# First layer of a two-stage model on one core: the dense groups in another order, the recurrence's preparation between them, norms on 128 rows

## The chip, the cores and the metric

The kernel runs on one core of a Trainium2 chip. The metric is the device time of one execution in microseconds (us), the median of several runs. TensorE does the matmuls, VectorE and ScalarE the elementwise work (ScalarE also the functions such as exp and gelu), GpSimd builds masks, and SyncE issues the loads from HBM. Each engine runs its own instructions strictly in the order in which they are written; they meet at semaphores.

## The reference

The input is one sequence of 512 tokens with 1024 channels. The change is in the mixer of the first layer; the 32-expert stage and the second model half behind it are not touched.

```
h = modulate(rmsnorm(x), shift1, scale1)          # shift1 and scale1 are columns of c @ ada_w + ada_b
z = h @ w_in                                      # split in zu, zv (512 each), then r, k, v (512 each), xw 32, xa 32, xg 96
# spatial half
u = gelu(zu);  v = layernorm(gelu(zv)) * ln_w + ln_b
y_a = u * (tril(ws) applied over the 128 tokens of a chunk, by head, to v, + bs)
# recurrent half: z + (z shifted by a token - z) * mu, then
decay = exp(-exp(-softplus(-(w0 + tanh(xw) @ w2)) - 0.5));  a = sigmoid(a0 + xa @ a2);  g = sigmoid(xg) @ g2
kk = k * k_k, divided by its norm over the 64 channels of a head;  k = k * (1 + (a - 1) * k_a)
state = state * decay + (state . -kk) (kk * a) + v k      # by head, token after token;  y = state . r
y_b = (norm of y by head * gn_w + gn_b + sum(r * k * r_k) * v) * g
x = x + gate1 * (concat(y_a, y_b) @ w_out)
```

## The kernel before

**Layout.** Activations lie transposed: channels on the 128 partitions, the 512 tokens along the row. A tile is 128 x 512; `R`, `K`, `V`, `KK`, `A` (the rate a), `C` (the decay) and `E` (scratch) have four tiles each. A chunk is 128 tokens. Eight heads of 64 channels make two heads per tile.

**Dense groups.** `PLAN` lists units of weights of at most 1 MB; SyncE loads them in that order into a ring of four slots. A `dense` group is 256 output channels: 2 x 8 x 3 = 48 matmuls of 128x128 by 512 (three because weight and activation are each split in a rounded high part and a rest). ScalarE writes the high part of a unit and VectorE the rest; the pair is called a *cut* here (`cut`, ordered by `Ahead`, which cuts a unit or two ahead of its use, and for which ScalarE waits until the unit two before it is used up). A group's result lies in one of two halves of `psD` in turn. For r, k, v and the two low-rank groups `lora_wa` and `lora_g` (24 matmuls each), ScalarE and VectorE each make a pass over the result (the token shift: L2150 or L2157, then L2333 or L2345).

**Small results.** Everything else that TensorE makes goes through `psA`, four banks in the fixed turn of `aux_plan`. TensorE waits on a bank until its previous content is taken.

**Order in the first layer.** Modulation rows (eight 1 MB units, `modulation`), their 16 columns (`to_column`), the norm, then the dense groups zv, zu, r, k, v, lora_wa, lora_g. Then comes the preparation of the recurrence: the low-rank products (`wl`, `al`), k times its factor, the squared norm of kk by head (`kn`, a product with the block matrix `blk`, so that all 64 rows of a head hold the same sum), root and reciprocal of it, the bonus (`bon`), the spatial mix (`gm`), the running sum of the decay, three exponentials, and the products `AR`, `A`, `K` that the chunks read. Then four chunks, each with seven levels of a block inversion, `u0`, `sa`, `y` and `st`. Last the norm of y by head (`gnm`, `gnv`), the gate `gg`, and the groups `w_out`. `keep_clock` runs matmuls whose result nobody reads.

Of the kernel before, what the change touches and what calls it, by code (L numbers as in the profile page):

```python
# [118 lines left out]
def gm2(a):  # L119
    out = np.zeros((P, 4, 512), np.float32)  # L120
    bs = np.asarray(a["gmlp_bs"][0])
    for j in range(4):
        for o in range(2):
            out[64 * o:64 * o + 64, 0, P * j:P * j + P] = bs[2 * j + o]
    out[0:32, 1] = np.asarray(a["rwkv_w2"][0])
    out[32:64, 2] = np.asarray(a["rwkv_a2"][0])
    out[0:96, 3] = np.asarray(a["rwkv_g2"][0])
    return out.reshape(P, UNIT)
# [12 lines left out]
def dense_plan():  # L141
# [10 lines left out]
    for j in range(8):  # L152
        mat(("ada", j), "ada_w", 0, cols(256 * j, 256 * j + 256))
    for h in range(2):
        mat(("zv",), "w_in", 0, cols(512, 1024), 4 * h, 4)
    for name, lo in (("zu", 0), ("r", 1024), ("k", 1536), ("v", 2048)):
        for j in range(2):
            mat((name, j), "w_in", 0, cols(lo + 256 * j, lo + 256 * j + 256))
    mat(("lora_wa",), "w_in", 0, cols(2560, 2624))
    mat(("lora_g",), "w_in", 0, cols(2624, 2720))  # L160
# [56 lines left out]

GROUPS = [g for g in dict.fromkeys(p[0] for p in PLAN) if g[0] not in ("ada", "zv")]
GROUPS = [("zv", 0), ("zv", 1)] + [q for g in GROUPS for q in ([(*g, h) for h in range(4)] if g[0] == "ple_w" else [g])]
# [3 lines left out]
def aux_plan():  # L223

    a = [("mr", 0, 0), ("mr", 0, 1), ("ss", 1)] + [("mr", 0, j) for j in range(2, 8)] + [("mod",)]
    a += [("wl", j) for j in range(4)] + [("al", j) for j in range(4)]
    a += [("kn", j) for j in range(4)] + [("bon", j) for j in range(4)]
    a += [("gm", c) for c in range(4)]
    for c in range(NCH):
# [13 lines left out]
        a += [("u0", c), ("sa", c), ("y", c)] + ([("st", c)] if c < NCH - 1 else [])  # L243
    a += [("gnm", j) for j in range(4)] + [("gnv", j) for j in range(4)] + [("gg", j) for j in range(4)]
# [72 lines left out]
def build(nc, x_t, params, w_dense, p_t, w_moe, out_t, stop=None):  # L317
    ctx = ExitStack()
    with ctx:
# [41 lines left out]
        X, H, YC = area(0, 8), area(4096, 8), area(8192, 8)  # L361
        XF, HF, YF = flat(0, 4096), flat(4096, 4096), flat(8192, 4096)
        o = 12288
        R, K, V, KK, A, C, E = (area(o + 2048 * i, 4) for i in range(7))
        RF, KF, VF, KKF, AF, CF, EF = (flat(o + 2048 * i, 2048) for i in range(7))
# [5 lines left out]
        T1 = area(sp + 1536, 1)  # L371
        NB = area(sp, 4)
        small = flat(sp + 4864, 512)
        stat = small[:, 0:4]
        AR = HF.rearrange("p (j c a t) -> p j c a t", j=4, c=4, a=2)
# [71 lines left out]
        g1_at, g2_at = ((RAW + 2 * (SPLIT_NO[last_unit((g,))] % 2)) * UNIT for g in ("lora_g", "lora_wa"))  # L447
# [3 lines left out]
        VTMP = flat(sp + 2816, 2048)  # L451
# [5 lines left out]
        YC_P = parts(o, o + 4 * 2048, 8)  # L457
        XI, XT = EF[:, 0:1024], EF[:, 1024:2048]
        AB = RF.rearrange("p (h a t) -> p h a t", h=8, a=2)
        AK = KKF.rearrange("p (h a t) -> p h a t", h=8, a=2)  # L460
# [184 lines left out]
        def moe_pool(pool, step):  # L645

            partial_sum(pool, step, [YC[:, k, :] for k in range(6)], PRE2, "sq2", 0)
# [39 lines left out]
        def moe_act(act, step, root, ahead, x_hi):  # L687

            for k in range(KT):
                act.wait_ge(sem("x_mixed"), k + 1)  # L690
                act.activation(YC[:, k, :], X[:, k, :], ACT.Square).then_inc(sem("sq2"), 1)
# [307 lines left out]
        def moe_tensor(pe, aux, filled, dense, colsum, product, keep_clock, spread):  # L999
            out = aux(("ss", 2))  # L1000
            for k, src in enumerate([PRE2, YC[:, 6, :], YC[:, 7, :]]):
# [994 lines left out]
        def _(sp_):  # L1996
            sp_.dma_start(XF, x_t).then_inc(sem("x_in"), 16)
            sp_.dma_start(par[:, :], params).then_inc(sem("par_in"), 16)

# [12 lines left out]
            for i in range(N_FIRST):  # L2012
                load(i)
                if PLAN[i][0] == ("lora_g",):

                    for n, g in ((1, "lora_wa"), (0, "lora_g")):
                        at = g1_at if n == 0 else g2_at
                        sp_.wait_ge(sem("units_done"), last_unit((g,)) + 1)
# [13 lines left out]
        def _(pool):  # L2032
# [17 lines left out]
            for i, m in enumerate(level):  # L2050
# [7 lines left out]
                                        pattern=[[2 * b, P // (2 * b)], [0, b]], channel_multiplier=-1))  # L2058
            pool.nop().then_inc(sem("consts"), 1)
# [6 lines left out]
            pool.wait_ge(sem("v_centred"), 1)  # L2066
            for m in range(4):
                step(pool.tensor_tensor(VTOK[:, m, :], VTOK[:, m, :], G1[:, 1024:1536], ALU.mult))
                pool.tensor_tensor(VTOK[:, m, :], VTOK[:, m, :], G1[:, 1536:2048], ALU.add)\
                    .then_inc(sem("v_norm"), 1)  # L2070
# [9 lines left out]
        def _(act):  # L2080
# [19 lines left out]
            ahead.limit = last_unit(("lora_g",))  # L2100
# [5 lines left out]
            act.activation(YF, XF, ACT.Square).then_inc(sem("sq1"), 1)  # L2106
            act.wait_ge(sem("par_in"), 16)
# [12 lines left out]
            ahead(last_unit(("zv",)))  # L2120

# [6 lines left out]
            for h in range(2):  # L2128
                ahead.enter(("zv", h))
                group_ready(act, ("zv", h))  # L2130
                act.activation(VTOK[:, 2 * h:2 * h + 2, :], dbank(("zv", h)), ACT.Gelu_apprx_tanh)\
                   .then_inc(group_freed(("zv", h)), 1)
            ahead.leave(("zv", 1))
            for h in range(2):
                ahead.enter(("zu", h))
                group_ready(act, ("zu", h))
                act.activation(YC[:, 2 * h:2 * h + 2, :], dbank(("zu", h)), ACT.Gelu_apprx_tanh)\
                   .then_inc(group_freed(("zu", h)), 1)
                ahead.leave(("zu", h))
            root(small[:, 48:52])  # L2140
# [710 lines left out]
```

## Time and profile before

| | us |
|---|---|
| median of 3 runs | 2892.51 (2889.79 to 2893.48) |
| the profiled execution, its own time | 2894.15 |
| its span in the trace | 2892.4 |
| TensorE busy in the span | 2665.4 (92%) |
| VectorE busy | 1576.2 (54%) |
| ScalarE busy | 1143.5 (40%) |
| mean granted TensorE clock | 0.955 |

The span is cut into 40 slices in the profile; a slice is 72.3 us long. The first layer takes the first eight and a half of them. The lines below the head are the busy share of each slice in tenths and the granted clock in tenths of full speed:

```
PE   7884999679999999989988799999999999999998
DVE  2248555547888888854357654333345474333334
PEclk8986999899999999999998899999999999999999
```

A digit says how busy an engine is, not whether anyone waits for it; waits are read in the timeline of the engine.

### The profile page before, as it was taken

What the parts mean: (1) busy time and instruction counts of PE and PEld (TensorE: products, weight loads), DVE (VectorE), ACT (ScalarE), POOL (GpSimd) and SP (SyncE); (2) the same over time, 40 slices, a digit from 0 to 9 for tenths busy, and PEclk for the clock granted to TensorE, in tenths of its full rate; (3) what the DMA queues carried; (4) which work ended last, traced back from release to release, by engine and by line L of the source; (5) the groups of instructions that cost most, each with busy time, mean ns of one, the idle gap of its engine ahead of it and who ended that gap; (6) DMA issues with size and microseconds to landing.
All of it is one profiled execution on the core that took longest, in us unless ns stands there. A gap on an engine that the chain in (4) does not pass through costs nothing.

```text
span 2892.4 us, 30835 instructions
## 1 busy us (share of the span) xinstructions
PE 2665.4 (92%) x12700; PEld 2081.9 (72%) x12700; DVE 1576.2 (54%) x1683; ACT 1143.5 (40%) x1322; POOL 152.1 (5%) x160
## 2 busy tenths in 40 slices
PE   7884999679999999989988799999999999999998
PEld 5653888457778878868865576888877756888876
DVE  2248555547888888854357654333345474333334
ACT  3231122235777778742231423222224364222223
POOL 1010000012111111000000000000010001000010
PEclk8986999899999999999998899999999999999999
DMA  6120222027999999952220122222232201223220
GB/s 251 55 88 15 73 74 74 0 88 270 361 361 361 361 352 363 357 209 81 95 78 11 55 77 71 88 90 102 75 108 81 79 1 66 98 71 115 80 102 30
DMA packets 64285, 388.06 MB, mean 134 GB/s; under 512 B 13328, under 2 KB 13456, under 8 KB 22288
## 3 DMA queue, kind: packets, MB, share of 16 engines
q1 hardware_dynamic: 53424, 372.41, 35.2%
q0 software_dynamic: 9280, 8.42, 0.8%
q10 hardware_dynamic: 1440, 5.24, 0.5%
q8 instruction: 102, 1.67, 0.2%
q14 instruction: 39, 0.32, 0.0%
HBM read 390.21 MB, written 20.97 MB: 142 GB/s over the span
## 4 chain that ended last, share of the span: by engine, by line
PE 76%; DVE 8%; ACT 3%; DMA 2%; issue 2%; DVEq 0%; ACTq 0%; POOLq 0%
PE psD L2579 60%; PE psA L2740 2%; DMA ring<-w_moe 2%; PE psA L2760 2%; PE psA L2754 1%; PE psA L1910 1%; DVE arena L2442 1%; PE psA L1039 1%; DVE ring_r L920 1%; PE psA L1941 1%; ACT ring_r L718 1%; PE psD L2587 1%; DVE ring_r L2279 1%; PE psA L2648 1%; PE psA L2587 1%
## 5 line engine op out<-in xcount | busy, mean ns | idle before, releaser
L2579 PE MATMUL psD<-rounded,ring_r 128*128 128x512 f32 (+1 forms) x6168 | 1456.7, 398 | 48.0 <-DVE ring_r L2279 25.3
L2579 PEld LDWEIGHTS psD<-rounded,ring_r 128*128 128x128 f32 (+1 forms) x6168 | 1158.9, 188 | 345.0 <-issue 34.9
L2279 DVE TENSOR_TENSOR ring_r<-ring,ring_r 128x2048 fp32r<-128x2048 f32 (+2 forms) x143 | 306.8, 2147 | 249.7 <-ACT ring_r L2097 245.6
L2579 PE MATMUL psD<-ring_r,rounded 128*128 128x512 f32 (+1 forms) x1728 | 410.6, 394 | 6.5 <-DVE rounded L930 3.3
L2097 ACT ACTIVATE ring_r<-ring 128x2048 fp32r<-128x2048 f32 (+2 forms) x143 | 251.7, 1761 | 397.0 <-PE psD L2579 366.6
L2579 PEld LDWEIGHTS psD<-ring_r,rounded 128*128 128x128 f32 x1728 | 318.1, 190 | 87.9 <-issue 9.1
L920 DVE TENSOR_TENSOR ring_r<-ring,ring_r 128x2048 fp32r<-128x2048 f32 x128 | 293.2, 2291 | 45.6 <-ACT ring_r L718 43.1
L718 ACT ACTIVATE ring_r<-ring 128x2048 fp32r<-128x2048 f32 x128 | 245.3, 1917 | 59.4 <-DMA ring<-w_moe 35.0
L2579 PE MATMUL psD<-rounded,rounded 128*128 128x512 f32 x768 | 191.7, 398 | 0.0
L1702 DVE TENSOR_TENSOR arena<-arena,psD 128x512 f32<-128x512 f32 x44 | 30.2, 687 | 255.2 <-ACT arena L1418 255.2
L920 DVE TENSOR_TENSOR rounded<-ring,rounded 128x2048 fp32r<-128x2048 f32 x64 | 146.5, 2289 | 23.6 <-ACT rounded L718 23.6
L2579 PEld LDWEIGHTS psD<-rounded,rounded 128*128 128x128 f32 x768 | 139.6, 188 | 27.3
L1418 ACT ACTIVATE arena<-psD 128x512 f32<-128x512 f32 x44 | 26.4, 599 | 307.9 <-PE psD L2579 307.9
L718 ACT ACTIVATE rounded<-ring 128x2048 fp32r<-128x2048 f32 x64 | 123.0, 1922 | 11.7 <-DMA ring<-w_moe 11.0
L2482 DVE TENSOR_TENSOR arena<-arena,psA 128x512 f32<-128x512 f32 x88 | 60.5, 688 | 66.0 <-PE psA L2754 47.8
L637 POOL TENSOR_TENSOR arena<-arena 128x512 f32<-128x512 f32 x5 | 7.5, 1507 | 1682.7 <-DVE arena L1675 1296.4
L2202 ACT ACTIVATE arena<-psA 128x512 f32<-128x512 f32 x56 | 33.4, 597 | 149.6 <-PE psA L2740 149.6
L2103 ACT ACTIVATE rounded<-arena 128x512 fp32r<-128x512 f32 x112 | 67.3, 627 | 61.0 <-DVE arena L1702 36.5
L1675 DVE SCALAR_TENSOR_TENSOR arena<-arena,psD 128x512 f32<-128x512 f32 x40 | 27.5, 686 | 78.7 <-PE psD L2579 78.0
L631 POOL DMA_INDIRECT pair_rows<-arena,ints x32 | 36.2, 1132 | 510.3 <-ACT arena L734 493.1
L2740 PE MATMUL psA<-arena 128*128 128x128 f32 x384 | 52.5, 285 | 1.6 <-DVE arena L2469 1.0
L2760 PE MATMUL psA<-arena 128*128 128x128 f32 x384 | 50.5, 276 | 0.0
(388 smaller groups left out, 2420.8 us busy)
## 6 DMA issues: line engine op xcount, KB each, us to landing
ring<-w_moe SPq DMA_DIRECT2D x192, 1024.0 KB, 7.3
ring<-w_dense SPq DMA_DIRECT2D x134, 1024.0 KB, 4.8
ring<-w_dense SPq DMA_DIRECT2D x16, 768.0 KB, 4.0
ring<-w_dense SPq DMA_DIRECT2D x16, 640.0 KB, 3.7
arena<-x_t SPq DMA_DIRECT2D x1, 2048.0 KB, 8.8
token_rows<-arena ACTq DMA_DIRECT2D x4, 512.0 KB, 2.6
arena<-pair_rows SPq DMA_DIRECT2D x4, 512.0 KB, 7.8
arena<-pair_rows ACTq DMA_DIRECT2D x4, 512.0 KB, 8.2
```

What stands on the lines that cost most here:

```text
L631: return pool.indirect_dma_start(pair_rows, bass.IndirectOffsetOnAxis(ap=pair_i[:, e:e + 1], axis=0), buf, None, bounds_check=2 * SEQ - 1, ...
L718: act.activation(expert_parts(E.place(j, PARTS))[0], slot_tile(slot), ACT.Copy).then_inc(sem("m_hi"), 1)
L920: dve.tensor_tensor(lo_, slot_tile(E.place(j, RAW)), hi, ALU.subtract).then_inc(sem("m_lo"), 1)
L2097: act.activation(parts_of(u, nk, nco)[0], ring_of(u, nk, nco), ACT.Copy).then_inc(sem("w_hi"), 1)
L2103: act.activation(dst, src, ACT.Identity if kw else ACT.Copy, **kw).then_inc(sem("x_hi"), 1)
L2202: act.activation(UI[:, 512 * q:512 * q + 512], bank(("u", c, lv, q)), ACT.Copy)\
L2279: dve.tensor_tensor(lo_, ring_of(u, nk, nco), hi, ALU.subtract).then_inc(sem("w_lo"), 1)
L2482: dve.tensor_tensor(buf[:, qs], buf[:, qs], bank(n_), ALU.add).then_inc(freed(n_), 1)
L2579: mm = pe.matmul(out, w[a], x[b], start=start and i == 0, stop=stop_ and i == 2)
L2587: pe.matmul(bank_, ones, masks[:, 0:SEQ], start=True, stop=True)
L2740: mm = pe.matmul(out[:, P * i:P * i + P], hs(LM[lv % 2], 4 * q + i), ident if lv == 0 else hs(XI, 4 * q + i), start=True, stop=True)
L2760: mm = pe.matmul(out[:, P * i:P * i + P], hs(UI, 4 * q + i), hs(XT, 4 * q + i), start=True, stop=True)
```

## The change

It reorders the first layer and rewrites its two norms by head.

- `PLAN`, and with it loads, cuts and matmuls, now goes k, lora_wa, r, v, lora_g, zv, zu. ScalarE and VectorE write the first two cuts between the tiles of `h1`, where both stood ahead of them.
- The preparation stands between the groups in all three engines' orders, and the exponentials come after the second v group. The factor -exp(-0.5) is now the scale of the exponentials.
- The norms by head: `by_head` gathers the sums of all eight heads and four chunks on 128 rows of 128 columns (16 matmuls with 32 output columns), root and reciprocal run on that 128 x 128 tile once, a product with the mask `PICK` spreads it to 512 columns, and `to_heads` (four matmuls, results `ks` and `gns`) brings it back to the channels.
- The 16 modulation columns are made two at a time behind each row. The 9 matmuls of `keep_clock` ahead of the first group are 3.
- The layer norm's scale and shift move from GpSimd to VectorE, with `ln_w` and `ln_b` loaded by a DMA of their own, which waits for the first four products of `AR`. A further small load (`WA2`, 256 KB) stands behind the parameters, and its end is waited for with them.
- GpSimd writes `PICK` and the map `HEADS` (7 small memsets and 4 copies of 32 x 512) before it signals `consts`, which TensorE's first matmul waits for.
- The gelu of zu, and the taking of `bon`, wait until all dense groups are done, since `YC` now lies over the split activations. The spatial mix of chunk k runs in the gaps at the end of recurrence chunks 0 and 1.

```diff
+    halves("k", 1536)
+    mat(("lora_wa",), "w_in", 0, cols(2560, 2624))
+    halves("r", 1024)
+    halves("v", 2048)
+    mat(("lora_g",), "w_in", 0, cols(2624, 2720))
     for h in range(2):
         mat(("zv",), "w_in", 0, cols(512, 1024), 4 * h, 4)
...
+    halves("zu", 0)
...
+            heads_map(HEADS)
             pool.nop().then_inc(sem("consts"), 1)
...
-                ready(dve, ("kn", j))
-                take(("kn", j), dve.tensor_scalar(NB[:, j, :], bank(("kn", j)), 1e-24, None, ALU.max))
-                counts_.append(ask_root())
...
-                inverse(counts_[j], NB[:, j, :])
-                step(dve.tensor_tensor(KK[:, j, :], KK[:, j, :], NB[:, j, :], ALU.mult))
...
+            def by_chunk():
+                inverse(ask_root(), NORM)
+                step(dve.tensor_tensor(NORM_C.rearrange("p (c t) -> p c t", c=NCH),
+                                       NORM.unsqueeze(1).to_broadcast([P, NCH, P]),
+                                       PICK[:, 0:NCH].unsqueeze(2).to_broadcast([P, NCH, P]), ALU.mult))
+                dve.nop().then_inc(sem("norm"), 1)
...
+            take(("kn",), dve.tensor_scalar(NORM, bank(("kn",))[:, 0:P], 1e-24, None, ALU.max))
+            by_chunk()
...
+            group_ready(dve, ("zu", 1))
+            for j in range(4):
+                ready(dve, ("bon", j))
+                take(("bon", j), dve.tensor_tensor(YC[:, 4 + j, :], bank(("bon", j)), V[:, j, :], ALU.mult))
...
+            def by_head(name, src, signal):
+                out = aux(name)
+                for j in range(4):
+                    pe.wait_ge(sem(signal), j + 1 if signal == "gn_sq" else 1)
+                    for c in range(NCH):
+                        mm = pe.matmul(out[32 * c:32 * c + 32, 0:P], PICK[:, 32 - 2 * j:64 - 2 * j],
+                                       src[:, j, P * c:P * c + P], start=(j == 0), stop=(j == 3))
+                filled(mm)
...
+            dense(("k", 0), hr, at="h1")
+            dense(("k", 1), hr)
+            dense(("lora_wa",), hr, (64,))
+            dense(("r", 0), hr)
+            by_head(("kn",), E, "kk_sq")
...
+            dense(("r", 1), hr)
+            to_heads("ks", HEADS, 1)
+            dense(("v", 0), hr)
...
+            dense(("v", 1), hr)
+            dense(("lora_g",), hr, (96,))
...
+            pe.wait_ge(sem("v_norm"), 4)
             pe.wait_ge(sem("bk"), 8)
...
-                inverse(counts_[j], NB[:, j, :])
-                step(dve.tensor_tensor(E[:, j, :], E[:, j, :], NB[:, j, :], ALU.mult))
-                step(dve.tensor_scalar(E[:, j, :], E[:, j, :], pc("gn_w", j), pc("gn_b", j), ALU.mult, ALU.add))
-                step(dve.tensor_tensor(YC[:, 4 + j, :], YC[:, 4 + j, :], E[:, j, :], ALU.add))
...
+                take(n_, dve.scalar_tensor_tensor(E[:, j, :], E[:, j, :], pc("gn_w", j), bank(n_),
+                                                  ALU.mult, ALU.mult))
+                step(dve.scalar_tensor_tensor(YC[:, 4 + j, :], E[:, j, :], pc("gn_b", j), YC[:, 4 + j, :],
+                                              ALU.add, ALU.add))
```

TensorE before, from the last matmuls of the last dense group (L2579) to the first chunk (L2718 on): wl, al, kn, bon and gm follow each other.

```order
L2579 MATMUL psD<-rounded_8_57,ring_r 96x512
L2694 MATMUL psA<-arena,ring 128x512 x4
L2696 MATMUL psA<-arena,ring 128x512 x4
L2699 MATMUL psA<-arena,masks 128x512 x4
L2702 MATMUL psA<-arena,masks 128x512 x4
L2708 MATMUL psA<-ring,arena 64x128 x32
L2718 MATMUL psA<-masks,arena 128x128 x12
L2728 MATMUL psA<-arena 128x256 x16
```

TensorE now, at four places of the dense stretch: the rows around the end of the first r group (by_head L2716, wl L2732, al L2734), of the second r group (ks L2723), of the first v group (bon L2740), and of the last dense group zu.

```order
L2606 MATMUL psD<-rounded_8_57,ring_r 128x512
L2716 MATMUL psA<-arena 32x128 x16
L2732 MATMUL psA<-arena 128x512 x4
L2734 MATMUL psA<-arena 128x512 x4
L2606 MATMUL psD<-rounded_8_57,ring_r 128x512
...
L2723 MATMUL psA<-arena 128x512 x4
...
L2740 MATMUL psA<-arena,masks 128x512 x4
...
L2606 MATMUL psD<-rounded_8_57,ring_r 128x512
L2774 MATMUL psA<-masks,arena 128x128 x12
L2784 MATMUL psA<-arena 128x256 x16
```

What stood in one row of small products behind the groups stands in three places between them; behind the last group the chunks' first products follow at once.

VectorE before, in the preparation: the norm of kk (L2260 the reciprocals; the last two of its four repeats are left out).

```order
L2260 RECIPROCAL arena<-arena 128x512 [waits aux_free1,root_out]
L2373 TENSOR_TENSOR arena<-arena 128x512 [waits dve_step]
L2374 TENSOR_TENSOR arena<-arena 128x512 [waits dve_step]
L2260 RECIPROCAL arena<-arena 128x512 [waits root_out,dve_step]
L2373 TENSOR_TENSOR arena<-arena 128x512 [waits dve_step]
```

VectorE now, from the shift of the first r group on: a cut (L2299) stands ahead of the norm, the reciprocal is 128 columns wide, and the shift of the second r group (L2337) follows the work on K.

```order
L2337 SCALAR_TENSOR_TENSOR arena<-psD,par,arena 128x511 [waits shift_a] x2
L2299 TENSOR_TENSOR ring_r<-ring,ring_r 128x2048 [waits shift_b,w_hi]
L2370 TENSOR_SCALAR arena<-psA 128x128 [waits aux_ready]
L2280 RECIPROCAL arena<-arena 128x128 [waits aux_free1,root_out]
L2356 TENSOR_TENSOR arena<-arena 128x512 [waits dve_step]
L2374 TENSOR_SCALAR arena<-arena,par,gain 128x512 [waits dve_step,aux_free2]
L2376 TENSOR_TENSOR arena<-arena 128x512 [waits dve_step]
```

The four wide reciprocals are gone, and the norm is now queued behind a cut, and a shift behind the norm.

## Rows read from the trace of the kernel before

**Rows 1.** Busy time by stage: columns are stretch, length, engines, granted clock, DMA.
```profile
0.00:52.50 52.50, 34.89 (x211) 20.82 (x211) 17.71 (x22) 22.35 (x27) 10.09 (x39) 0.84 0.81 329
52.50:189.50 137.00, 125.75 (x530) 98.13 (x528) 36.44 (x40) 33.39 (x35) 0.00 (x0) 0.96 0.12 44
189.50:272.90 83.40, 34.21 (x140) 19.44 (x140) 71.73 (x80) 23.46 (x27) 12.12 (x9) 0.65 0.16 63
272.90:526.50 253.60, 231.25 (x2012) 213.60 (x2012) 126.76 (x168) 51.46 (x93) 0.00 (x0) 0.93 0.20 67
526.50:564.10 37.60, 17.41 (x40) 7.52 (x41) 32.43 (x31) 10.95 (x17) 0.00 (x0) 0.80 0.00 0
```

**Rows 2.** Timeline of TensorE (start, length, instructions, wait before), 0 to 130 us.
```profile
13.35 1.94 PE L2648 MATMUL psA<-ring,par 128*32 128x256 f32 x16 [13.35 <-DMA ring<-w_dense]
...
17.20 7.13 PE L2628 MATMUL psA<-arena,masks 128*128 128x512 f32 x16
...
33.45 1.94 PE L2648 MATMUL psA<-ring,par 128*32 128x256 f32 x16 [0.50 <-DMA ring<-w_dense]
...
36.01 6.96 PE L2659 MATMUL psA<-gain,arena 128*128 128x1 f32 x32 [0.57 <-ACT arena L2112]
...
76.56 22.66 PE L2579 MATMUL psD<-rounded,ring_r 128*128 128x512 f32 x96 [1.11 <-ACT arena L2131]
```

**Rows 3.** Timeline of GpSimd, 0 to 285 us.
```profile
3.69 0.53 POOL L2041 MEMSET reset<- 128x512 f32 x1
...
12.63 0.24 POOL L2057 TENSOR_SCALAR_AFFINE_SELECT masks<-masks 128x64 f32<-128x64 f32 x1
...
196.01 1.26 POOL L2069 TENSOR_TENSOR arena<-arena,ring 128x512 f32<-128x512 f32 x1
```

**Rows 4.** Timeline of ScalarE, 0 to 285 us.
```profile
43.49 0.81 ACT L2124 ACTIVATE arena<-arena,mod,gain 128x512 f32<-128x512 f32 x1 [3.30 <-DVE gain L2302]
44.34 0.63 ACT L2103 ACTIVATE rounded<-arena 128x512 fp32r<-128x512 f32 x1
...
132.99 1.27 ACT L2150 ACTIVATE arena<-psD,gain 128x512 f32<-128x512 f32 x2 [8.07 <-PE psD L2579]
134.14 1.91 ACT L2097 ACTIVATE ring_r<-ring 128x2048 fp32r<-128x2048 f32 x1
144.19 1.27 ACT L2150 ACTIVATE arena<-psD,gain 128x512 f32<-128x512 f32 x2 [8.13 <-PE psD L2579]
...
189.60 1.28 ACT L2163 ACT_TABLE_LOAD   x1
```

**Rows 5.** Timeline of VectorE, 0 to 285 us.
```profile
136.09 2.29 DVE L2279 TENSOR_TENSOR ring_r<-ring,ring_r 128x2048 fp32r<-128x2048 f32 x1 [0.97 <-ACT ring_r L2097]
...
239.06 5.00 DVE L2388 TENSOR_TENSOR_SCAN arena<-reset,arena 128x512 f32<-128x512 f32 x4
```

**Rows 6.** Timeline of TensorE, 130 to 275 us.
```profile
231.46 5.50 PE L2702 MATMUL psA<-arena,masks 128*128 128x512 f32 x8 [21.98 <-DVE arena L2379]
236.89 3.71 PE L2708 MATMUL psA<-ring,arena 128*64 128x128 f32 x64
260.29 1.09 PE L2718 MATMUL psA<-masks,arena 128*128 128x128 f32 x4 [19.69 <-DVE arena L2428]
```

**Rows 7.** Timeline of VectorE, start of the first and the second chunk.
```profile
272.86 2.36 DVE L2454 TENSOR_TENSOR arena<-arena,masks 128x1024 f32<-128x1024 f32 x2
...
334.08 5.77 DVE L2442 TENSOR_TENSOR arena<-psA,masks 128x512 f32<-128x512 f32 x8 [0.95 <-PE psA L2728]
```

**Rows 8.** Chain of work that ended last, in order of time, 340 to 350 us.
```profile
347.42 1.00 PE psA L2648 x16
```

**Rows 9.** Timeline of VectorE, 510 to 582 us.
```profile
534.51 3.35 DVE L2260 RECIPROCAL arena<-arena 128x512 f32<-128x512 f32 x1
...
556.20 2.85 DVE L2529 TENSOR_TENSOR arena<-arena,psA 128x512 f32<-128x512 f32 x4
```

**Rows 10.** Chain of work that ended last, 560 to 612 us.
```profile
564.12 47.53 PE psD L2579 x192
```

More of the change, by code:

```diff
@@ L2099, in _ @@
             ahead = Ahead(cut)
-            ahead.limit = last_unit(("lora_g",))
+            ahead.limit = last_unit(("zu", 1))
             def x_hi(dst, src, **kw):
@@ L2221, in _ @@
                 act.activation(C[:, j, :], E[:, j, :], ACT.Square).then_inc(sem("gn_sq"), 1)
-            for j in range(4):
-                root(NB[:, j, :])
+            root(NORM)
             act.wait_ge(sem("y_halves"), 2)
@@ new lines, in to_heads @@
+            def to_heads(name, heads, count):
+                pe.wait_ge(sem("norm"), count)
+                for j in range(4):
+                    filled(pe.matmul(aux((name, j)), heads[:, P * j:P * j + P], NORM_C, start=True, stop=True))
+            dense(("k", 0), hr, at="h1")
[3 more added lines that the diff above has]
+            by_head(("kn",), E, "kk_sq")
+            pe.wait_ge(sem("lora_w"), 1)
+            for j in range(4):
+                filled(pe.matmul(aux(("wl", j)), WA2[0:32, P * j:P * j + P], LO[0:32, 0, :], start=True, stop=True))
@@ L2683, in _ @@
-            hr = tile_of(H_P)
-            for name in ("zu", "r", "k", "v"):
-                for h in range(2):
-                    dense((name, h), hr)
-            dense(("lora_wa",), hr, (64,))
-            dense(("lora_g",), hr, (96,))
-            g2, ws = G2, G1[:, 0:1024].rearrange("p (h t) -> p h t", h=8)
-            pe.wait_ge(sem("gm2_in"), 16)
-            pe.wait_ge(sem("lora_w"), 1)
-            for j in range(4):
-                filled(pe.matmul(aux(("wl", j)), g2[0:32, 1, P * j:P * j + P], LO[0:32, 0, :], start=True, stop=True))
@@ L2704, in _ @@
-            for c in range(4):
-                pe.wait_ge(sem("v_norm"), c + 1)
-                out = aux(("gm", c))
+                for b in range(2):
+                    if i == 0:
+                        pe.wait_ge(group_freed(("zv", b)), GROUP_NO[("zv", b)] // 2)
+                    for k in range(nk):
+                        for m in (2 * b, 2 * b + 1):
+                            mm = product(psD[:, GROUP_NO[("zv", b)] % 2, m % 2, :],
+                                         [v[:, 4 * i + k, P * m:P * m + P] for v in H_P],
+                                         [v[:, k, :] for v in w], i == 0 and k == 0, i == 1 and k == nk - 1)
```

378 lines of the change are left out of this document (204 added, 174 removed).

## The prediction

> **What bounds the kernel now.** I read the busy time by stage first, since the change touches only the first 611 us. Up to 52.5 us the loads of the modulation weights and the first norm set the pace. From 52.5 to 189.5 us TensorE is busy 125.8 of 137 us at a granted clock of 0.96: the dense groups. From 189.5 to 272.9 us it is busy 34.2 of 83.4 us at 0.65, while VectorE is busy 71.7: the preparation, bound by VectorE. Then come the chunks (TensorE 231 of 254), and from 526.5 to 564.1 the norm of y, where VectorE is busy 32.4 of 37.6 us [rows 1]. The timelines say who waits: TensorE waits 22.0 us for VectorE ahead of the bonus and 19.7 us ahead of the first chunk's transposes [rows 6]. In both norms a reciprocal of 128x512 stands four times on VectorE, one takes 3.35 us [rows 9]. The dense groups run evenly: ScalarE takes up a group's result every 11.20 us (132.99 to 144.19), so a matmul of 512 columns takes 11.2/48 = 0.233 us, a group of 24 takes 5.6 [rows 4].
>
> **Can the preparation lie under the groups?** By total work, yes. VectorE had 36.4 us to do in the groups' stage and 71.7 in the preparation's [rows 1]; three quarters of four reciprocals go (4 x 3.35 x 0.75 = 10 us). That leaves about 98 us for some 140 us of TensorE work. Totals don't decide it, though: the queues are strictly ordered, and a cut that is late stops TensorE. So I walked them.
>
> **Start.** TensorE's first matmul began at 13.35 us, when its weights had landed [rows 2]. It now waits for GpSimd, whose last mask ended at 12.87 [rows 3], and then 7 small memsets (0.2 us each, since the 64-column mask takes 0.24) and 4 copies of 512 columns. The trace has no such copy: at least the 0.53 us of the 512-column memset, at most the 1.26 of an operation with two inputs [rows 3]; between ends this near, I take 0.9. TensorE starts at about 18 (16.4 to 19.5), 4.6 later. The last modulation row moves from 33.45 to 38.1. Behind it 32 column instructions took 6.96 us [rows 2]; 4 are left, 0.9. With the row's 1.94, its copy and VectorE's two small operations, h1 begins at 42.2 instead of 43.5 [rows 4]. ScalarE then has 8 tiles of 0.81 + 0.63 us and 2 cuts of 1.91 (15.2 in all); the rest of the last tile 0.7 and six matmuls 1.4 make the first k group end at 59.4.  Next k (11.2), lora_wa (5.6), r (11.2, with 0.3 lost to a cut that ends late): the first r group ends at T = 87.7.
>
> **From T on.** Cover and delays, in us after T; shift on ScalarE 1.27, cut 1.91 and 2.29 [rows 4, 5].
> ScalarE ends shift and cut at 3.4, VectorE its cut at 5.7. Only then does VectorE take the gathered norm. Root, a reciprocal of 128 columns (3.35/4 = 0.84) and the mask end at 8.0. ScalarE, after the root, reloads its table (1.28 [rows 4]) and takes wl and al one by one, since the four banks turn; TensorE is through with them at 12.0, where its own work alone (gathering 2.0, eight products at 7.13/8 = 0.89 [rows 2]) was 9.1: a wait of 2.9. Gathering is 32 instructions of at most 32 output columns; 16 such take 1.00 in the chain [rows 8], so 2.0.
> Second r group to 23.2, ks (4 x 0.89) to 26.8, v to 38.0, bonus to 41.6, v to 52.8, lora_g to 58.4. VectorE meanwhile has r times r_k times k and the products with ks (done at 37.5), the four scans (5.00 [rows 5]) and the two passes behind them, done at 51.8, just ahead of the second v group's result. The exponentials follow that group's shift and cut: three at 1.9 and a table, ending at 63.2. ScalarE reaches the shift of lora_g only then, and zv's second half needs that half of psD: TensorE waits 0.8 at 64.3. zv ends at 81.9. The gelu of zv holds zu up by 1.3, much like the 1.11 wait before [rows 2]. zu ends at 105.6. The layer norm is done at 98.7 (cut, 4 statistics, root, 8 products of 0.72), so it is covered, with 7 us to spare; without that cover each us counts in full. TensorE is free for the chunks at 87.7 + 105.6 = 193.3.
>
> **What is late next.** The banks hold the bonus until zu is done. VectorE takes four (2.9), then come the eight takings of ab and ak (5.8 [rows 7]) and their lead of 1.4: the first level mask starts at 193.3 + 10.1 = 203.4. Before it started at 272.86 [rows 7]. **Gain 69.5.**
>
> **Inside the chunks.** Four spatial products of 3.71/4 = 0.93 us [rows 6] go where TensorE waits for ScalarE's copy of u0 or sa anyway. That costs between nothing and 3.7; nearer nothing, as the copy is already waited for: I charge 1.0. VectorE's part lies under sa and y. GpSimd's second four copies may hold VectorE up: 0 to 4 us, I take 0.5. The fresh clock at the first chunk may give up to 3; I take 0 to 3 into the range only.
>
> **Norm of y.** From the first reciprocal's start at 534.51 to the end of the gate products at 556.20 + 2.85 = 559.05 are 24.5 us [rows 9]. Now: reciprocal 0.84, mask 0.72, first product 0.89 and hand-off 0.2, four times two passes (5.8), gate 2.85: 11.3. That is 13.2 less, and the gathering (2.0 under the squares, instead of 4 x 0.89) starts the chain 0.9 earlier: **14.1**. Then w_out: its 192 matmuls took 47.53 [rows 10], where four groups at 11.2 are 44.8. In the stage ahead of them TensorE was busy 17.4 of 37.6 us, at a mean clock of 0.80 [rows 1]. Now keep_clock's matmuls end within 1 us of them: **2.7** more.
> In the Trainium skill, "TensorE: Matmul & The Clock Gate" (Part 1) says the array runs at half rate by default and that activity releases it; the trace agrees, by the 47.53 against 44.8.
>
> **Sum.** 69.5 - 1.0 - 0.5 + 14.1 + 2.7 = 84.8. The profiled execution took 2894.15 (span 2892.4 and 1.75 around it), so 2809.4; it stood 1.6 above the median of 2892.51. That gives 2807.8; I put 1 us back for hand-offs not walked: **2809 us**, 2.9% less.
>
> **Rivals.**
> *Late hand-offs* (0.17). The cut waits behind other work on both queues. If it comes one pair late (1.91 + 2.29 = 4.2 us [rows 4, 5]) at six of the eight remaining groups, 25 us come back: 2834. For it: the preparation's operations depend on each other and VectorE stands at 70%. Against: cuts run a group ahead.
> *Clock dips* (part of the forecast's case). Narrow products and the 2.9 us wait stand between groups; the preparation's stage had 0.65 [rows 1]. One dip costs what w_out lost, 2.7; three, 8: 2817.
> *Switching the array* (0.04). Gathering uses a quarter of the columns and wl and al a quarter of the rows, so TensorE changes form six times. If each change drained it for one product of 0.89 [rows 2], 5 us would go: 2814. Against: a 32-column row takes 1.00 in the chain amid full products [rows 8].
> The Trainium skill, "TensorEngine Tiling (Array Packing)" (Key Properties), says that changing the tiling mode drains TensorE, which speaks against this change; it gives no figure.
> *No overlap* (0.06). If a chain through the preparation ended where it did, only the narrower norms would count: 10 us in the preparation, 16.8 at y: about 2866.
> *Slower* (0.03). TensorE's clock falls to 1.2 GHz early in the broken-up stretch and stays. Each of 528 matmuls then costs 0.233 more, 123 us: 2932. It decides from 85/0.233 = 365 matmuls on, seven and a half groups. Against: the groups' stage kept 0.96 over 137 us and 530 matmuls [rows 1].
> *The change does nothing* (0.02): some wait, such as the second small load behind the last cut, restores the old end; 2892.
>
> **How the numbers follow.** The forecast has 0.68 (2799 to 2820; ends from the start's +-1.6, the chunks' +3 and -4, three dips). The range runs to the late hand-offs: 2798 to 2836. A measurement can tell about 0.2%, 6 us, from no change: faster 0.95, the same 0.02, slower 0.03.
>
> **What the profile will show.** Right: first chunk's level mask near 203, TensorE's longest wait under 3 us between 60 and 193, the level norm's 128-column reciprocals under 1 us, w_out from about 479 and done in about 45 us. Wrong: waits of 4 us for cuts ahead of several groups, a granted clock under 0.9 between 60 and 190, or a gap between zu's end and the chunks over 4 us.

## The result, and the profile after

The kernel after the change takes 2809.82 us (median of 4 runs, 2806.46 to 2813.14) against 2891.95 of before on the same chip: ratio 0.9716, 95% interval 0.97 to 0.9733. The prediction was 2809. The profiled execution took 2806.46 us, its span is 2804.4; before's was 2892.4.

Busy time by stage of the kernel after, cut where the stages of [rows 1] end (loads and norm; groups with the preparation between them; to the first chunk's mask; four chunks; norm of y):
```profile
0.00:47.40 47.40, 27.34 (x198) 16.09 (x198) 12.62 (x17) 15.35 (x19) 13.22 (x50) 0.93 0.80 309
47.40:197.60 150.20, 146.08 (x592) 105.50 (x592) 82.27 (x102) 60.07 (x63) 0.00 (x0) 0.95 0.26 91
197.60:207.70 10.10, 7.21 (x45) 5.60 (x44) 8.31 (x13) 3.49 (x5) 1.09 (x1) 1.00 0.30 104
207.70:459.00 251.30, 232.60 (x2077) 215.13 (x2077) 132.36 (x176) 51.46 (x93) 2.43 (x4) 0.94 0.20 68
459.00:483.70 24.70, 20.74 (x72) 8.67 (x73) 16.48 (x22) 9.09 (x14) 0.00 (x0) 0.93 0.00 1
```
The groups and the preparation were 137 and 83.4 us one behind the other; now they are one stage of 150.2 us in which TensorE is busy 146.1 and VectorE 82.3. VectorE's 36.4 and 71.7 us of [rows 1] have become 82.3 and 8.3, most of it now beside TensorE's work.

Timeline of TensorE after (start, length, instructions, wait before), answering [rows 2] and [rows 6]:
```profile
16.76 2.35 PE L2675 MATMUL psA<-ring,par 128*32 128x256 f32 x19 [16.76 <-POOLq L2086]
...
37.69 1.69 PE L2675 MATMUL psA<-ring,par 128*32 128x256 f32 x16 [1.66 <-DMA ring<-w_dense]
...
47.40 8.66 PE L2606 MATMUL psD<-rounded,ring_r 128*128 128x512 f32 x36 [1.64 <-DVE ring_r L2299]
56.66 31.28 PE L2606 MATMUL psD<-rounded,ring_r 128*128 128x512 f32 x132 [0.59 <-DVE rounded L2306]
87.87 1.08 PE L2716 MATMUL psA<-arena 128*32 128x128 f32 x32
88.88 2.84 PE L2732 MATMUL psA<-arena 32*128 32x512 f32 x6
93.62 2.07 PE L2732 MATMUL psA<-arena 32*128 32x512 f32 x2 [1.90 <-DVE arena L2370]
96.02 7.19 PE L2734 MATMUL psA<-arena 32*128 32x512 f32 x8 [0.33 <-ACT arena L2182]
103.14 12.88 PE L2606 MATMUL psD<-rounded,ring_r 128*128 128x512 f32 x48
115.86 3.59 PE L2723 MATMUL psA<-arena 128*128 128x512 f32 x8
...
174.96 22.66 PE L2606 MATMUL psD<-rounded,ring_r 128*128 128x512 f32 x96 [1.11 <-ACT arena L2205]
198.50 1.69 PE L2774 MATMUL psA<-masks,arena 128*128 128x128 f32 x9 [0.88 <-DVE arena L2441]
```
The two waits of 22.0 and 19.7 us are gone. So is a third, which lay inside the dense stretch of before, ahead of the first `r` group:
```profile
108.72 21.66 PE L2579 MATMUL psD<-rounded,ring_r 128*128 128x512 f32 x85 [9.50 <-DVE ring_r L2279]
```
The cut that it waited for stood on VectorE behind the layer norm of zv, and that waited 18.11 us for a root which ScalarE took up only behind the gelu of zu. In the new order the layer norm comes under zu, with no cut for `r` behind it.

Between 60 and 193 us the longest wait now is 1.90, ahead of `wl`'s last tile. The same product is not always equally quick, though (the trace shows each of these f32 products as two instructions): the four `al` products take 7.19 us, where the four `ks` products at 115.86 take 3.59. The granted clock says why; columns as in [rows 1]:
```profile
86.00:92.00 6.00, 5.72 (x47) 3.08 (x45) 2.33 (x3) 4.00 (x4) 0.00 (x0) 1.00 0.39 161
92.00:95.00 3.00, 1.38 (x2) 0.50 (x2) 2.53 (x4) 1.67 (x3) 0.00 (x0) 0.60 0.27 49
95.00:104.00 9.00, 8.68 (x11) 3.25 (x11) 4.40 (x7) 5.44 (x9) 0.00 (x0) 0.50 0.24 100
104.00:109.00 5.00, 5.00 (x18) 3.92 (x18) 1.24 (x2) 0.00 (x0) 0.00 (x0) 0.77 0.01 2
116.00:197.00 81.00, 79.74 (x328) 60.19 (x327) 54.62 (x68) 29.04 (x26) 0.00 (x0) 1.00 0.28 98
```
From the wait ahead of `wl`'s last tile until some 3.5 us into the second `r` group TensorE's granted clock is 1.2 instead of 2.4 GHz; before and behind, it is full.

Timelines of VectorE and of GpSimd, after, answering [rows 5, 7, 9] and [rows 3]:
```profile
94.00 0.95 DVE L2280 RECIPROCAL arena<-arena 128x128 f32<-128x128 f32 x1 [0.43 <-ACT arena L2113]
...
189.54 0.75 DVE L2436 SCALAR_TENSOR_TENSOR arena<-arena 128x512 f32<-128x512 f32 x1
197.66 2.87 DVE L2441 TENSOR_TENSOR arena<-psA,arena 128x512 f32<-128x512 f32 x4 [7.37 <-PE psD L2606]
201.88 5.77 DVE L2467 TENSOR_TENSOR arena<-psA,masks 128x512 f32<-128x512 f32 x8 [1.35 <-PE psA L2784]
207.68 2.36 DVE L2479 TENSOR_TENSOR arena<-arena,masks 128x1024 f32<-128x1024 f32 x2
...
465.80 0.95 DVE L2280 RECIPROCAL arena<-arena 128x128 f32<-128x128 f32 x1 [0.81 <-ACT arena L2113]
...
475.79 2.85 DVE L2556 TENSOR_TENSOR arena<-arena,psA 128x512 f32<-128x512 f32 x4
```
```profile
14.05 2.60 POOL L2082 COPY arena<-masks 32x512 f32<-32x512 f32 x4
```
VectorE is through with the preparation and the layer norm at 190.3 and then idle 7.37 us until the banks may be taken: the chain through the preparation ends ahead of TensorE's. The first level mask starts at 207.68 instead of 272.86: **65.2 us** of gain. The chunks take 251.3 us instead of 253.7 (first mask to `gnm`), 2.4 more; the norm of y 24.74 instead of 37.59 (`gnm` to `w_out`), 12.85 more; and `w_out` is a piece of 45.04 us on the chain, where [rows 10] had 47.53:
```profile
483.71 45.04 PE psD L2606 x192
```
These make 82.9 of the 88.0 us between the two spans. The other 5.1 lie behind `w_out`, in code that is the same in both. Over the ten profiled executions of this document that code takes 2272 to 2284 us, so 5.1 is no effect of the change. The chunks vary too: in the nine kernels that have the changed chunk code they take 246.2 to 255.9 us, so their 2.4 can't be put down to the change either.

### The profile page after: what moved, and what is told of

It is laid out like the page before. It is cut to its first block, busy times and chain, and to the rows that moved or that the text cites. A ratio compares the mean times of both kernels' runs of the same rounds, so it can differ in the third digit from the quotient of the medians.

```text
span 2804.4 us, 30921 instructions
## 1 busy us (share of the span) xinstructions
PE 2650.3 (95%) x12752; PEld 2069.1 (74%) x12752; DVE 1542.8 (55%) x1672; ACT 1141.7 (41%) x1318; POOL 146.9 (5%) x167
## 4 chain that ended last, share of the span: by engine, by line
PE 84%; DVE 7%; ACT 4%; DMA 2%; issue 2%; POOL 0%; DVEq 0%; ACTq 0%; SPq 0%; POOLq 0%
PE psD L2606 66%; PE psA L2796 2%; DMA ring<-w_moe 2%; PE psA L2816 2%; PE psA L2810 1%; PE psA L1921 1%; PE psA L2675 1%; PE psA L1050 1%; DVE arena L2467 1%; ACT ring_r L2122 1%; DVE ring_r L2299 1%; PE psA L1952 1%; PE psD L2614 1%; PE psA L2655 1%; DMA ring<-w_dense 1%
## 5 line engine op out<-in xcount | busy, mean ns | idle before, releaser
L2299 DVE TENSOR_TENSOR ring_r<-ring,ring_r 128x2048 fp32r<-128x2048 f32 (+2 forms) x143 | 307.1, 2147 | 239.4 <-ACT ring_r L2122 235.8
L2796 PE MATMUL psA<-arena 128*128 128x128 f32 x384 | 53.0, 287 | 1.0 <-DVE arena L2494 0.4
L2796 PEld LDWEIGHTS psA<-arena 128*128 128x128 f32 x384 | 47.8, 199 | 3.9 <-issue 3.9
```

Source lines behind the costliest of these rows:

```text
L2299: dve.tensor_tensor(lo_, ring_of(u, nk, nco), hi, ALU.subtract).then_inc(sem("w_lo"), 1)
L2796: mm = pe.matmul(out[:, P * i:P * i + P], hs(LM[lv % 2], 4 * q + i), ident if lv == 0 else hs(XI, 4 * q + i), start=True, stop=True)
```

## The experiments

All compute the whole reference; where TensorE gets additional matmuls, nobody reads their results. Between kernels whose medians are a few us apart the ratio can't decide, since their intervals overlap with that of the changed kernel (0.97 to 0.9733); there the argument rests on a stretch of the trace. Each was timed beside the kernel before on the same chip (2888.04 us in experiments 1, 2, 4 and 5, 2892.36 in the others), so ratios are compared. "Gathering to mask" is the time from the start of `kn`'s products, at 87.87 us after the change, to the first chunk's level mask: 119.81 us after the change.

**1. Filling TensorE's waits** (x1_fill). Two idle products of 512 columns (four instructions) stand before `wl`'s last tile and two before `al`, behind a wait for the half of `psD` that they write.
```diff
             for j in range(4):
+                if j == 3:
+                    keep_clock(psD[:, 0, 0, :], 2)
                 filled(pe.matmul(aux(("wl", j)), WA2[0:32, P * j:P * j + P], LO[0:32, 0, :], start=True, stop=True))
+            keep_clock(psD[:, 0, 0, :], 2)
```


> Against the changed kernel (2809.8 us, profiled span 2804.4). There TensorE waits 1.90 and 0.33 us at wl and al, the granted clock is 0.50 from 95 to 104 us, al takes 7.19 us for four products and the second r group ends at 115.9. Four idle 128x512 matmuls now stand in these waits, in a half of psD that is free. Theory 'clock': the waits cost mostly by the clock that they let fall; with the waits filled al takes about 4 and the r group 11.3, so the group ends near 111 and the first chunk's mask starts near 203 instead of 207.7: 4.8 us less, 2805. Rival 'turn of the banks': the hand-overs to ScalarE set the pace of wl and al whatever the clock; the mask stays at 207 to 208 and the time at 2809 to 2811. If the fillers are themselves late, up to 1 us more.

Ratio 0.9714 (0.9695 to 0.9733), 2805.86 us. Gathering to mask is 115.48 us, 4.3 less; `al` takes half as long and the `r` group 11.46. Timeline of TensorE, then windows:
```profile
92.03 1.12 PE L2735 MATMUL psA<-arena 32*128 32x512 f32 x2
93.08 1.98 PE L2614 MATMUL psD<-masks 128*128 128x512 f32 x4
95.00 3.69 PE L2738 MATMUL psA<-arena 32*128 32x512 f32 x8
98.62 11.46 PE L2606 MATMUL psD<-rounded,ring_r 128*128 128x512 f32 x48
```
```profile
92.00:95.00 3.00, 3.00 (x8) 0.98 (x7) 1.64 (x2) 2.90 (x5) 0.00 (x0) 1.00 0.73 216
```
The idle products kept the clock at 1.00. That fits two readings: the waits took the clock, or the narrow products did, and fillers help against both. The gain shows on the path but is too small for the ratio to tell (0.9714 against 0.9716).

**2. The low-rank products behind the second `r` group** (x2_lowrank_later). Nothing is added; `wl` and `al` move, and with them their work on ScalarE and VectorE.
```diff
             by_head(("kn",), E, "kk_sq")
+            dense(("r", 1), hr)
             pe.wait_ge(sem("lora_w"), 1)
...
-            dense(("r", 1), hr)
             to_heads("ks", HEADS, 1)
```


> Against the changed kernel. wl and al, with ScalarE's and VectorE's work on them, go behind the second r group, so that the norm has freed its bank long before. Theory 'queue order' (the wait came from where wl stands, and the slow clock from the wait): by_head is followed at once by the r group, which ends near 100; wl and al then wait for ScalarE's shift, cut and table load and end near 109.5, ks near 113, the first v group near 124 instead of 130.5; the mask starts near 201.5, 2803.6 us. Rival 'it only moves': the wait for ScalarE behind the r group is as long and the clock falls there: mask within 1.5 us of 207.7, no gain.

Ratio 0.9723 (0.9703 to 0.9743), 2805.86 us; gathering to mask 118.69, 1.1 us less where my theory wanted 6. Timeline, then windows:
```profile
100.13 4.51 PE L2733 MATMUL psA<-arena 32*128 32x512 f32 x8
105.35 7.19 PE L2735 MATMUL psA<-arena 32*128 32x512 f32 x8 [0.72 <-ACT arena L2183]
112.47 5.70 PE L2723 MATMUL psA<-arena 128*128 128x512 f32 x8
```
```profile
98.00:102.00 4.00, 4.00 (x15) 2.34 (x14) 1.04 (x2) 1.76 (x3) 0.00 (x0) 1.00 0.01 2
102.00:103.50 1.50, 1.50 (x4) 0.57 (x3) 0.53 (x2) 1.48 (x2) 0.00 (x0) 0.79 0.00 0
105.40:112.50 7.10, 7.10 (x9) 2.47 (x9) 3.49 (x7) 3.70 (x6) 0.00 (x0) 0.50 0.43 149
```
The theory falls. `wl` no longer waits, and the clock still drops, at 0.79 over 102 to 103.5 us, while TensorE is busy all 1.50 us of it; the first wait (0.72) comes behind the drop. The dip moved along with the narrow products. What these have of their own is that they contract over 32 of the 128 rows.

**3. The same products over 128 rows** (x8_rows128). The rows that a product doesn't need are zeros; `al`'s weights get a tile of their own, with a load of 256 KB behind `lora_wa`'s units, and GpSimd writes the zeros of the activation before `consts`. Order and waits stay.
```diff
-                filled(pe.matmul(aux(("wl", j)), WA2[0:32, P * j:P * j + P], LO[0:32, 0, :], start=True, stop=True))
+                filled(pe.matmul(aux(("wl", j)), WA2[:, P * j:P * j + P], LO[:, 0, :], start=True, stop=True))
...
-                filled(pe.matmul(aux(("al", j)), WA2[32:64, P * j:P * j + P], LO[32:64, 0, :], start=True, stop=True))
+                filled(pe.matmul(aux(("al", j)), WA3[:, P * j:P * j + P], LO[:, 0, :], start=True, stop=True))
```


> Against the changed kernel. wl and al contract all 128 rows (the 32 rows of weights in a matrix that is zero elsewhere, the unused rows of the activation set to zero), in the same place, with the same waits; a 256 KB load more, well ahead, and one GpSimd memset of about 0.5 us before the constants. When the two products stood behind the second r group, the granted clock fell to 0.50 about 3 us after them had begun, with TensorE busy throughout. Theory 'narrow rows': 32-row products do not keep the clock up; on 128 rows it stays at 1.00 through the 1.9 us wait, al takes about 3.7 instead of 7.19 and the r group 11.4 instead of 12.7, from by_head's start to the first level mask 115.5 us instead of 119.8, as with the waits filled. Rival 'the waits': the 1.90 and 0.33 us waits let the clock fall, rows don't matter: 119.8 again, al 7.2.

Ratio 0.971 (0.969 to 0.9729), 2805.33 us; gathering to mask 114.78, 5.0 us less. Timeline and windows:
```profile
94.47 1.12 PE L2735 MATMUL psA<-arena 128*128 128x512 f32 x2 [1.90 <-DVE arena L2373]
96.96 3.67 PE L2738 MATMUL psA<-arena 128*128 128x512 f32 x8 [1.36 <-ACT arena L2185]
100.07 11.76 PE L2609 MATMUL psD<-rounded,ring_r 128*128 128x512 f32 x48
```
```profile
92.00:95.00 3.00, 1.10 (x3) 0.30 (x2) 2.57 (x3) 1.67 (x3) 0.00 (x0) 1.00 0.00 0
95.00:98.60 3.60, 2.23 (x6) 0.87 (x5) 1.49 (x2) 3.59 (x6) 0.00 (x0) 1.00 0.81 291
```
This settles it for this place. Both waits are there, the second even longer, TensorE is busy only 1.10 of 3 us, and the clock stays at 1.00 throughout. After the change the same stretch had it busy 1.38 us and the clock at 0.60. Here the narrow rows take the clock, not the waits. In the time the 5 us don't show clear of noise (0.971 against 0.9716).

**4. GpSimd and the start** (x3_consts_early). TensorE's first wait is released ahead of GpSimd's new memsets and copies; only `by_head` and `to_heads` wait for those.
```diff
+            pool.nop().then_inc(sem("consts"), 1)
             step(pool.memset(PICK, 0.0))
...
+                pe.wait_ge(sem("consts"), 2)
```


> Against the changed kernel. GpSimd signals the constants before the seven small memsets and four copies for PICK and HEADS; by_head waits for them. Theory 'start': TensorE's first matmul moves from 16.76 to about 14.1 (weights landed, a 256 KB load later than the 13.35 of before), the last modulation row from 37.7 to about 34.4, everything behind it by 3.2 us: mask near 204.5, 2806.6 us. Rival 'loads set the start': the last row waits 1.66 us for its weights, whose load is issued when an earlier unit is done, so at most that wait changes and the gain is under 1 us.

Ratio 0.9729 (0.9711 to 0.9747), 2809.18 us. Timeline of TensorE:
```profile
15.59 1.93 PE L2676 MATMUL psA<-ring,par 128*32 128x256 f32 x16 [15.59 <-DMA ring<-w_dense]
```
The start comes 1.2 us earlier and is then set by the first unit of weights, which landed by 13.35 us before the change. The load of `WA2` (128x512 in f32, 256 KB) now stands ahead of it. TensorE also waits for the end of that load itself, but it had landed by 12.84, when VectorE, which waits for it too, began. The mask comes at 206.82, 0.9 earlier. My theory, a start at 14.1 and 3.2 us of gain, falls, and the rival (loads set the start, under 1 us) holds. So GpSimd hid a second delay of 2.2 us, and taking GpSimd's away alone gives 0.9 us.

**5. The norm of y as before** (x5_wide_y_norm). The sums come from `blk` for all 64 rows of a head, with four roots and four reciprocals of 512 columns, and the three passes by tile behind them where the change has two; all else as changed.
```diff
-            by_head(("gnv",), C, "gn_sq")
+            for j in range(4):
+                pe.wait_ge(sem("gn_sq"), j + 1)
+                filled(pe.matmul(aux(("gnv", j)), blk, C[:, j, :], start=True, stop=True))
...
+            for j in range(4):
+                inverse(counts_[j], NB[:, j, :])
```


> Against the changed kernel. The norm of y goes back to the form of before: four products with blk, four reciprocals of 128x512. All else as changed. Theory 'the narrow norm is worth its chain': the stretch from the start of gnm to the last gate product, 19.7 us in the changed kernel and 32.5 before, goes back to 32.5, and w_out's 192 matmuls from 45.0 to 47.5: 15.3 us more, 2825. Rival 'the gain there came from the order': without the narrow norm less than 8 us come back, under 2818.

Ratio 0.9771 (0.9751 to 0.979), 2822.77 us: 0.0055 of 2888 us is 16 us slower than the changed kernel. `gnm` starts at 455.05 and `w_out` 37.59 us later, to the hundredth as before. Timeline of VectorE, and the chain:
```profile
479.30 3.35 DVE L2282 RECIPROCAL arena<-arena 128x512 f32<-128x512 f32 x1
```
```profile
492.64 47.35 PE psD L2609 x192
```
12.85 for the norm and 2.3 for the clock of `w_out`: the new form of the norm of y (narrow root and reciprocal, one pass by tile less) is worth 15.2 us.

**6. The whole preparation behind the groups** (x6_prep_behind). Order k, r, v, zv, zu, then the preparation; the norms stay narrow.
```diff
-            by_head(("kn",), E, "kk_sq")
-            pe.wait_ge(sem("lora_w"), 1)
...
-            to_heads("ks", HEADS, 1)
...
+            by_head(("kn",), E, "kk_sq")
+            pe.wait_ge(sem("lora_w"), 1)
...
+            to_heads("ks", HEADS, 1)
```


> Against the changed kernel. All dense groups, their shifts, the gelu of zv and the layer norm stay in the new order; the whole preparation (factor on k, narrow norm, wl, al, ks, bonus, scans, exponentials, the products for the chunks) goes behind zu on all three engines. Theory 'order': TensorE ends its groups near 174, and the preparation with the narrow norm stands open with some 50 us of VectorE work less what lies under TensorE's, so the first level mask starts at 232 to 238 instead of 207.7: 24 to 30 us more, 2834 to 2840. Rival 'the narrow norms did it': the mask moves by less than 10 us.

Ratio 0.9811 (0.9791 to 0.983), 2834.94 us, 27 us slower than the changed kernel (0.0095 of 2892). The mask comes at 239.11, 31.4 later, of which 2.9 arose ahead of the first dense product (50.30 instead of 47.40). Timeline of TensorE:
```profile
180.26 1.93 PE L2716 MATMUL psA<-arena 128*32 128x128 f32 x32 [3.92 <-ACT arena L2193]
...
228.37 2.79 PE L2774 MATMUL psA<-masks,arena 128*128 128x128 f32 x12 [23.56 <-DVE arena L2438]
```
The wait for VectorE is back. Putting the preparation *between* the groups is thus worth 28.5 us at the mask (31.4 less 2.9), at the upper end of what I expected. It is less than half of the 65.2. This kernel's mask still comes 33.8 us ahead of before's: 2.2 from the start; 10.3 in the groups (126.1 us against 136.4), nearly all of it the wait of 9.50 for a cut that the new order of the groups doesn't have; and 21.2 in the preparation (62.8 us against 84.0), with the narrow norm of kk and without the spatial mix. What each of these two gives wasn't isolated.

**7. The norm of kk wide, in the new order** (x4_wide_kk_norm).
```diff
-            by_head(("kn",), E, "kk_sq")
+            pe.wait_ge(sem("kk_sq"), 1)
+            for j in range(4):
+                filled(pe.matmul(aux(("kn", j)), blk, E[:, j, :], start=True, stop=True))
...
-            to_heads("ks", HEADS, 1)
```


> Against the changed kernel. The norm of kk in the form of before (four products with blk, four roots and four reciprocals of 128x512, no ks), in the new order. Theory 'covered': VectorE gets 12.5 us more of reciprocals, but they lie under the second r group, and TensorE loses the four ks products (3.6 us): from by_head's start to the first level mask 117 to 122 us instead of 119.8, time 2807 to 2813. Rival 'on the path' (10 us in the preparation, as in the prediction's case without overlap): 127 or more, 2817 or more.

Ratio 0.9736 (0.9712 to 0.9761), 2816.46 us (2804.74 to 2819.37). From `kn` to the mask it takes 120.58 us against 119.81, as the theory had it. In these 0.8 us TensorE saves the four `ks` products (3.6 us), and spends 2.5 more on `kn` (3.60 against 1.08) and 0.8 more in the wait ahead of `wl` (2.74 against 1.90); the 10 us more of reciprocals on VectorE hardly show, since groups cover them. The median, though, is 3 us above the 2807 to 2813 that I expected and near the rival's 2817, and its interval overlaps with the changed kernel's, so the time doesn't decide. The profiled execution lost more in the first chunk, 67.15 us against 62.66. Windows of the last third of the first chunk, of this kernel:
```profile
252.00:275.45 23.45, 21.05 (x156) 19.27 (x156) 10.22 (x15) 3.37 (x6) 0.00 (x0) 0.78 0.01 1
```
and of the kernel after:
```profile
251.00:270.34 19.34, 16.75 (x161) 14.99 (x160) 10.63 (x16) 3.37 (x6) 0.00 (x0) 0.99 0.01 2
```
Nearly the same work (the windows begin 0.4 us apart in it) runs 4.1 us longer at a clock of 0.78. The kernel before had 0.79 there as well (23.88 us). So the clock of that stretch isn't set by the stretch alone; what sets it stays open.

**8. The pieces together** (x9_best). The fillers of experiment 1, the early release of experiment 4, `WA2` loaded behind the units of `lora_wa`, and three idle products while the norm of y waits for its root.
```diff
-            sp_.dma_start(WA2, w_dense[len(PLAN) + 1][:, 512:1024]).then_inc(sem("par_in"), 16)
...
+                if i == last_unit(("lora_wa",)):
+                    sp_.dma_start(WA2, w_dense[len(PLAN) + 1][:, 512:1024]).then_inc(sem("wa_in"), 16)
...
+                if count == 2:
+                    pe.wait_ge(sem("pair_free0"), 6)
+                    keep_clock(psD[:, 0, 0, :], 3)
```


> Against the changed kernel. The fillers in the waits of wl and al, constants signalled ahead of PICK and HEADS, the small weight load moved from behind the parameters to behind the unit of lora_wa, and three idle matmuls while TensorE waits for the norm of y. Theory 'sum of parts': TensorE starts at 13.4 again, the last modulation row at 33.5 to 34.5, so h1 begins 3 us earlier; 4.3 from the clock at wl and al; about 1 from gns at full clock: 8 us less, 2802 if the changed kernel is at 2810. Rival 'the loads take it back': the last row waits for its weights as before, whatever TensorE's start, and only 5 us come.

Ratio 0.9686 (0.9666 to 0.9706), 2799.2 us: 0.003 of 2892 is 8.7 us less than the changed kernel, the best version here, though the intervals overlap a little. Timeline of TensorE:
```profile
13.14 1.93 PE L2677 MATMUL psA<-ring,par 128*32 128x256 f32 x16 [13.14 <-DMA ring<-w_dense]
...
44.09 6.10 PE L2608 MATMUL psD<-rounded,ring_r 128*128 128x512 f32 x25 [0.85 <-DVE ring_r L2301]
```
The start is 3.6 us earlier, the first dense product 3.3, the mask 7.65 (200.03), the norm of y 0.8 shorter. The last modulation row comes 2.5 us earlier, at 35.20; I expected 33.5 to 34.5, and it waits for its weights as the rival said, but more than that rival's 5 us came in all. With `WA2` out of the way the first weights land where they did before the change, which confirms experiment 4's reading. What the idle products in the norm of y are for shows in the kernel after, in the `gns` products of `to_heads`:
```profile
467.64 5.37 PE L2723 MATMUL psA<-arena 128*128 128x512 f32 x8 [3.01 <-issue]
```
There the granted clock is 0.67 over 467.6 to 472.8 us; with the idle products it is 1.00 and the same four take 3.70. No product over 32 rows stands near, so a clock can also fall around a wait of 3 us; whether the wait or the gathering onto 32 columns ahead of it takes it here wasn't isolated.

## Why the prediction was right, point by point

**The mechanism** held. The preparation lies under the groups, its chain ends 7.4 us ahead of TensorE's, and experiment 6 shows that this placing is worth 28.5 us at the mask, experiment 5 that the norm of y and its clock are worth 15. The wait of 9.50 us in the groups of before, which the new order takes away, I walked past without naming it ("the dense groups run evenly").

**Start.** 18 predicted, 16.76 measured: the copy takes 0.65 us where I took 0.9 between 0.53 and 1.26. The last modulation row comes at 37.69 (38.1), T at 87.9 (87.7). I named GpSimd and missed that the new load held the weights back as well (experiments 4 and 8). That the row and T came so close is partly luck: I moved the row by as much as the start (4.6), but it waits 1.66 us for its own weights and doesn't follow the start one to one. In experiment 4 the start is 1.2 us earlier and the row 0.9, in experiment 8 it is 3.6 and 2.5.

**From T to the second `r` group** one term was mis-sized: "one dip costs what w_out lost, 2.7". Low-rank products end at T + 15.3 instead of 12.0, the second `r` group at T + 28.0 instead of 23.2. The 4.8 us are all clock. In experiment 3, with its clock kept, the same points are T + 11.35 and T + 22.9, so the walk of the queues was sound. Gathering takes 1.08 us instead of 2.0: the products of [rows 8] by which I priced it run over 256 columns, these over 128. Of the wait of 2.9 I was right in place and a little high (1.90 and 0.33). The dip was put down to "the 2.9 us wait" and to narrow products alike; here it is the latter alone.

**From there to the mask** the walk held within a microsecond: zv ends 58.0 us later (58.7 predicted, the wait of 0.8 didn't occur), zu waits 1.11 (1.3) and ends at T + 109.8, the mask follows 10.1 us later (10.1). The gain at the mask is 65.2 and not 69.5: 4.8 of clock less 0.8 of the wait make up nearly all of it.

**Chunks.** I charged 1.5; they gained 2.4. The first takes 62.66 us (67.02 before) at a granted clock of 0.97 instead of 0.87, within the up to 3 us I kept for the range and 1.4 more. Windows of the first two chunks after:
```profile
207.68:270.34 62.66, 58.24 (x532) 53.51 (x532) 35.87 (x48) 13.26 (x24) 0.00 (x0) 0.97 0.20 68
270.34:335.24 64.90, 60.92 (x556) 56.35 (x556) 36.58 (x49) 13.26 (x24) 2.43 (x4) 0.95 0.19 66
```
The second took 64.42 before, at a clock of 0.97 instead of 0.95: 32 more matmul instructions (spatial products) and GpSimd's four copies cost 0.5 us together at most, a third of my charge. Experiment 7 shows that the first chunk's 4.4 can be lost again by a clock dip in its last third, so no design can count on it. With 246.2 to 255.9 us for the four chunks in one and the same code, neither my charge nor their gain can be confirmed.

**Norm of y.** 14.1 predicted, 12.85 measured by the change's own trace and 12.85 again by experiment 5. From the reciprocal's start to the end of the gate products it takes 12.84 us and not 11.3: the first product back comes at the lower clock (1.65 us to its taking instead of 1.1), and the four pairs of passes take 6.5 instead of 5.8. Between the gathering and the first product back to the channels TensorE stands still for 3.01 us (take, root, reciprocal, mask). `w_out` gained 2.5 of 2.7.

**The sum.** 2809 against 2809.82 is closer than the terms are. The mask came 4.3 us short of the forecast, the norm of y and `w_out` 1.5, and the chunks made up 3.9, which they could as well have not. Of the signs that I named as wrong, one occurred: the granted clock is 0.95 over 60 to 190 us as a whole, but 0.50 for nine us of it.

**The rivals.** *Late hand-offs*: no wait for a cut in the whole stage beyond 1.64 us at its very beginning (the 0.59 behind it is for a tile of `h1`). *Clock dips*: between the groups one, of 4.8 us, not three of 2.7; the one at `gns` (5.37 us instead of 3.6) lies outside them. *Switching the array*: none to be seen; the 32 gathering matmuls take 1.08 us (2.0 predicted) and the low-rank ones start within it, at 88.88. The rule of the Trainium skill, "TensorEngine Tiling (Array Packing)" (Key Properties), that changing the tiling mode drains TensorE, costs nothing measurable here. *No overlap* and *nothing* are out by the mask at 207.68. *Slower*: the clock did fall, but rose again inside the next full group (0.77 over 104 to 109 us, 1.00 from there), far from the 365 matmuls at which that rival decides. This rise under full products agrees with the rule of the Trainium skill, "TensorE: Matmul & The Clock Gate" (Part 1), that activity releases the clock. Experiment 2 adds that being busy was not enough to hold it.

## What to carry to other kernels

When an engine waits through a long dependent chain, look for work that is free of it and stands in the same queue: put the chain's steps one by one *between* pieces of that work, and walk the queues, since totals say only that it may fit. Between full groups, try to pad matmuls over few rows with zero rows: here four products took 3.67 us over 128 rows and 3.69 over 32 at full clock, and only the former kept that clock without idle products beside them. A small load put ahead of the first big one delayed it by 2.2 us here; issue it where its reader is. Before crediting a few us to a change, look at how much a stretch of unchanged code varies between executions: here the chunks by 10 us and the rest behind `w_out` by 11.

## What the runs showed of the hardware

Products over 32 of 128 rows let the granted clock fall to 0.50 though TensorE was busy without a pause (experiment 2), and the same products over 128 rows kept 1.00 with TensorE busy 1.10 of 3 us (experiment 3). 32 matmul instructions onto 32 output columns took 1.08 us together at full clock and 1.93 at the lower one (experiment 6). A wait of 3.01 us behind such products went with a clock of 0.67 on the next ones, and three idle products in it kept 1.00 (experiment 8). Loading 256 KB ahead of the first unit of weights moved its landing from 13.35 to 15.59 us. One and the same chunk takes 62.7 or 67.2 us by the clock granted in its last third (0.99 or 0.78).
